# A decay series moved along VectorE's order, and three tiles' router scores computed during a square root

## The reference, cut to what matters

```python
x_r = part of x @ w_in                         # 1280 channels, 10 blocks of 128
xc = causal_dwconv(x_r, conv_r_w) + conv_r_b   # 4 taps
r_gate = sigmoid(block_diag(xc, w_rg_a, b_rg_a))
i_gate = sigmoid(block_diag(xc, w_rg_x, b_rg_x))
log_a = -8 * r_gate * softplus(-rg_lambda)     # the decay; softplus by a series here
a_t, b_t = exp(log_a), sqrt(-expm1(2 * log_a)) * (i_gate * xc)
h_r = linear_recurrence(a_t, b_t)
...
x = layer_norm(ALPHA * x + merged @ w_out)
logits = x @ w_router + b_router               # 16 scores a token
group = argmax over 4 groups of the sum of the two best probabilities
experts = the two best in that group
```

## Time and profile before

| what | value |
|---|---|
| median of 3 runs | 827.77 us (827.19 to 829.04) |
| the profiled execution | 826.91 us |
| its span, first to last instruction | 825.2 us |
| PE busy | 813.2 us, 99% |
| DVE busy | 575.2 us, 70% |
| ACT busy | 455.0 us, 55% |
| POOL busy | 81.9 us, 10% |

### The profile page before, as it was taken

One profiled execution on the slowest core, in us unless ns is written; L12 is line 12 of the kernel. 1 busy time (PEld: TensorE's weight loads), 2 busy tenths in 40 slices (PEclk: granted clock), 3 DMA queues, 4 the chain that ended last, 5 costly groups with the idle time before them and its releaser, 6 DMA issues.

```text
span 825.2 us, 11010 instructions
## 1 busy us (share of the span) xinstructions
PE 813.2 (99%) x3803; PEld 676.4 (82%) x3803; DVE 575.2 (70%) x672; ACT 455.0 (55%) x462; POOL 81.9 (10%) x78
## 2 busy tenths in 40 slices
PE   9999999999999999999999999999999999999996
PEld 8788888888888888888888888888888888888883
DVE  5877445434547886432455688898899989999977
ACT  5655524433466663432332434578787788887842
POOL 1000000100000000000000000551310001100027
PEclk9999999999999999999999999999999999999998
DMA  7232324653233333333532836499999999999692
GB/s 232 81 107 85 102 84 149 202 178 101 77 102 102 89 88 106 98 103 114 172 95 76 332 127 233 138 376 386 419 373 390 392 396 400 392 396 393 255 363 104
DMA packets 112358, 173.51 MB, mean 210 GB/s; under 512 B 7418, under 2 KB 90019, under 8 KB 100550
## 3 DMA queue, kind: packets, MB, share of 16 engines
q1 hardware_dynamic: 106502, 159.80, 54.7%
q0 software_dynamic: 5824, 13.30, 4.2%
HBM read 163.49 MB, written 16.30 MB: 218 GB/s over the span
## 4 chain that ended last, share of the span: by engine, by line
PE 86%; DMA 6%; DVE 5%; issue 1%; ACT 1%; DVEq 0%; SPq 0%; ACTq 0%
PE psA L718 8%; PE psA L720 8%; PE psA L719 8%; PE psB L718 6%; PE psB L719 6%; PE psB L720 6%; PE psA L905 5%; PE psA L907 5%; PE psA L906 5%; DMA est<-in_w_exp_down_dram 5%; DVE elo L1656 2%; PE psB L932 2%; PE psB L930 2%; PE psB L931 2%; PE psD L719 2%; PE psD L718 2%
## 5 line engine op out<-in xcount | busy, mean ns | idle before, releaser
L1656 DVE TENSOR_TENSOR elo<-est,ehi 128x2048 fp32r<-128x2048 f32 x94 | 212.4, 2288 | 26.1 <-ACT ehi L1254 26.0
L1254 ACT ACTIVATE ehi<-est 128x2048 fp32r<-128x2048 f32 x94 | 178.9, 1924 | 53.5 <-DMA est<-in_w_exp_down_dram 36.5
L1441 DVE TENSOR_TENSOR wlo<-wst,whi 128x1024 fp32r<-128x1024 f32 (+1 forms) x75 | 93.9, 1251 | 84.9 <-ACT whi L1081 84.2
L1081 ACT ACTIVATE whi<-wst 128x1024 fp32r<-128x1024 f32 (+1 forms) x75 | 80.9, 1078 | 76.9 <-PE psB L720 30.7
L905 PE MATMUL psA<-ehi,xe_hi 128*128 128x512 f32 x256 | 101.5, 397 | 0.2 <-issue 0.2
L907 PE MATMUL psA<-ehi,xe_lo 128*128 128x512 f32 x256 | 99.9, 390 | 0.0
L906 PE MATMUL psA<-elo,xe_hi 128*128 128x512 f32 x256 | 99.6, 389 | 0.0
L718 PE MATMUL psB<-xT_hi,whi 128*128 128x512 f32 x208 | 81.0, 390 | 0.0
L720 PE MATMUL psB<-xT_hi,wlo 128*128 128x512 f32 x208 | 80.9, 389 | 0.0
L719 PE MATMUL psB<-xT_lo,whi 128*128 128x512 f32 x208 | 80.9, 389 | 0.0
L907 PEld LDWEIGHTS psA<-ehi,xe_lo 128*128 128x128 f32 x256 | 48.0, 188 | 10.4
(11 more groups left out here) (374 smaller groups left out, 1532.7 us busy)
## 6 DMA issues: line engine op xcount, KB each, us to landing
est<-in_w_exp_gate_dram SPq DMA_DIRECT2D x32, 1024.0 KB, 11.0
est<-in_w_exp_up_dram SPq DMA_DIRECT2D x32, 1024.0 KB, 11.4
est<-in_w_exp_down_dram SPq DMA_DIRECT2D x32, 1024.0 KB, 12.9
wst<-in_w_in_dram SPq DMA_DIRECT2D x59, 512.0 KB, 3.9
wst<-in_w_branch_r_dram SPq DMA_DIRECT2D x8, 640.0 KB, 4.3
ys<-zero POOLq DMA_DIRECT2D x8, 512.0 KB, 2.9
wst<-in_w_branch_a_dram SPq DMA_DIRECT2D x8, 512.0 KB, 3.6
o_st<-in_w_out_dram SPq DMA_DIRECT2D x8, 512.0 KB, 4.3
```

The costliest lines, as they stand in the source:

```text
L1081: A(whi[p][:, 0:K, :], wst[p][:, 0:K, :], ACT.Copy).then_inc(w_hi, 1)
L1254: A(ehi[s][:], est[s][:], ACT.Copy).then_inc(gu_hi if s < 4 else d_hi, 1)
L1441: V.tensor_tensor(wlo[p][:, 0:K, :], wst[p][:, 0:K, :], whi[p][:, 0:K, :], ALU.subtract).then_inc(w_lo, 1)
L1656: V.tensor_tensor(elo[s][:], est[s][:], ehi[s][:], ALU.subtract).then_inc(gu_lo if s < 4 else d_lo, 1)
```

## The change

Three edits, all in DVE's order. Ahead of the loop, `decay_first` runs before `rg_rest(0)` and `rg_rest(1)`; `rg_rest(0)` comes behind the first convolution, `xc_rest(0)` ahead of `lo(2)`, `rg_rest(1)` behind `lo(2)`; and `decay_rest` comes behind the second convolution, its remainder, and the drive of block 0. `gates_of` is split in `decays` and `drive`. In the root, the scores of tiles 0 to 2 are computed between the last tile's variance and its reciprocal.

```diff
-            def gates_of(j, p):
+            def decays(j):
+                V.tensor_scalar(_tile(zbuf, j), _tile(zbuf, j), _col(decay[:, 0, :], 0, j), None, ALU.mult)
+
+            def drive(j, p):
                 dve.wait_ge(gate_done, j + 1)
-                V.tensor_scalar(_tile(zbuf, j), _tile(zbuf, j), _col(decay[:, 0, :], 0, j), None, ALU.mult)
                 V.tensor_tensor(_tile(ibuf, j), ig[p][:], xc[p][:], ALU.mult).then_inc(ix_done, 1)
 
-            rg_rest(0, 0)
-            rg_rest(1, 1)
             decay_first()
             conv_rest(0, 0)
+            rg_rest(0, 0)
+            xc_rest(0, 0)
             lo(2, 0)
-            xc_rest(0, 0)
-            decay_rest()
+            rg_rest(1, 1)
             conv_rest(1, 1)
             lo(3, 1)
             xc_rest(1, 1)
-            gates_of(0, 0)
+            drive(0, 0)
+            decay_rest()
+            decays(0)
...
-                    gates_of(2 * i + (p - 1), 1 - p)
+                    dve.wait_ge(gate_done, 2 * i + p)
+                    decays(2 * i + (p - 1))
+                    drive(2 * i + (p - 1), 1 - p)
...
+            def score(t):
+                return V.scalar_tensor_tensor(lb[:, t, :], logit_ps[t], st1[:, t, 18:19],
+                                              shift[:, t, :], ALU.mult, ALU.subtract)
+
             def norm(t):
...
+                if t == TT - 1:
+                    dve.wait_ge(logit_done, TT - 1)
+                    for u in range(TT - 1):
+                        score(u)
                 dve.wait_ge(std_done, t + 1)
...
-            for t in range(TT):
-                dve.wait_ge(logit_done, max(t + 1, TT - 1))
-                ins = V.scalar_tensor_tensor(lb[:, t, :], logit_ps[t], st1[:, t, 18:19],
-                                             shift[:, t, :], ALU.mult, ALU.subtract)
-            chain.link(ins)
+            dve.wait_ge(logit_done, TT)
+            chain.link(score(TT - 1))
```

More of the change, by code:

```diff
@@ L1529, in _ @@
                     xc_rest(2 * i + p, p)
-                    gates_of(2 * i + (p - 1), 1 - p)
+                    dve.wait_ge(gate_done, 2 * i + p)
+                    decays(2 * i + (p - 1))
+                    drive(2 * i + (p - 1), 1 - p)
             chain.n = start + 4 * (KR // 2 - 1)
-            gates_of(KR - 1, 1)
+            dve.wait_ge(gate_done, KR)
+            decays(KR - 1)
+            drive(KR - 1, 1)
             QC = KR * S // 4
@@ L1664, in residual @@
                 V.bn_stats(st1[:, t, 6 * h:6 * h + 6], row).then_inc(stats_done, 1)
+            lb = r16[2]
+            def score(t):
+                return V.scalar_tensor_tensor(lb[:, t, :], logit_ps[t], st1[:, t, 18:19],
+                                              shift[:, t, :], ALU.mult, ALU.subtract)
             def norm(t):
@@ L1764, in _ @@
             ex, iota3 = r16[1], iota_e[:].unsqueeze(1).to_broadcast([P, TT, NE])
-            lb, inside = r16[2], r16[4]
+            inside = r16[4]
             def beats(o, v):
```

## The result

Over 22 executions of each kernel the changed one takes 829.22 us in the median (828.07 to 829.80) and the kernel before 826.69 (826.09 to 829.04). The ratio is 1.0023, with a 95% interval of 1.0017 to 1.0029: slower by 1.9 us, or 1.4 to 2.4. The ratio isn't the quotient of the two medians, which lie 2.53 apart; the means, 829.11 and 827.21, lie 1.90 apart. The forecast was +1.9 and 829.7 us. The three executions that were shown ahead of the prediction lay high, with a median of 827.77. The profiled execution of the changed kernel took 829.5 us, its span 827.8.

The account below looks back on a forecast made before the run. TensorE, busy 99% of the span, was taken to bound the kernel. +2.24 us from the start and -0.33 from the scores made +1.9, added to the 827.77 median: 829.7 us, range 826.6 to 830.9.

Parts of the forecast that it names:

- a queue entry held up by rg_lo(0): SyncE's queue: weight tile 3's load waits behind a reload that needs rg_lo(0); new TensorE stop of about 1.8 us.
- the series without cover: VectorE, second half of the decay series ahead of the third convolution: TensorE stops again for 1.2 us.
- the gain at rg(0): First gate products on TensorE: the 0.82 us hole ahead of them goes, and they start at 22.43.
- the scores: Last tile's root: three scores (0.51 us) leave the chain, reciprocal 0.18 later; net -0.33, bounds -0.51 to 0.
- The issue of tile 3: SyncE issues weight tile 3's load at 21.89, not 17.32, 1.28 us behind the end of rg_lo(0).
- ScalarE's rounding: ScalarE rounds weight tile 3 once its load lands, at 26.0 (25.7 to 27.0), instead of 23.30.
- rg(1) and rg(2): Second and third starts of gate products on TensorE: at 31.0 and 39.1, 0.84 and 2.12 us later than before.
- Nothing late behind the first wait: Rival, chance 0.13: tile 3's weights come in time, third gate products start at 36.4; 827.0 us.
- Only the first new stop: Rival, chance 0.08: second half of the series finds cover, third gate products start at 37.9; 828.4 us.
- The table switch: Rival, chance 0.03: ScalarE's table load costs twice its 1.28 us in its new place; 831.0 us.
- The clock: Rival, chance 0.03: TensorE's clock falls in a 1.8 us stop; one round at 1.2 GHz costs up to 6.8; 836 us.
- The threshold: Whole kernel: 0.2%, or 1.66 us, tells from no change (829.4); slower has 0.54, within 0.43, faster 0.03.

Follow-up runs that it names:

- i1_best: Repeat of e6_best (changed kernel, rg_lo(0) ahead of the series, six of the second half's twelve operations moved earlier); 825.93 us, ratio 0.9990.
- i2_scores: Kernel before with the score edit alone, run again; 826.00 us, ratio 0.9989.
- g2_early: Changed kernel without the score edit, so VectorE's new order at the start alone; 829.44 us, ratio 1.0030.
- g3_spq: Changed kernel with only SyncE's loop altered: both weight tiles loaded ahead of both pairs of gate weights; 825.96 us, ratio 0.9984.
- e5_rg0: Changed kernel with rg_lo(0), the first small remainder of gate weights, back ahead of the series; 825.98 us, ratio 0.9988.
- g4_cover: Changed kernel with the series' second half cut in two, six operations ahead of tile 3's small remainder and six behind it; 827.88 us, ratio 1.0008.
- e6_best: Changed kernel with rg_lo(0) ahead of the series and six of the second half's twelve operations between the remainders of tile 3 and xc(1); 825.95 us, ratio 0.9989.
- h1_before16: Kernel before with 16 filler products instead of 12 on TensorE while the experts are chosen; 826.76 us, ratio 0.9993.
- e7_best8: e6_best with 8 filler products instead of 12 on TensorE while the experts are chosen; 826.62 us, ratio 0.9992.
- h2_before8: Kernel before with 8 filler products instead of 12 on TensorE while the experts are chosen; 827.12 us, ratio 1.0001.

## Why the prediction was right

- **The number and the mechanism.** The mechanism came as it was written: a queue entry held up by rg_lo(0), then the series without cover. That the number came so close is in part luck. The 829.7 was added up from the median of three executions, 827.77, which lies 1.08 above the median of 22, 826.69; the measured 829.22 is 2.53 above the latter. The +1.9 has two terms that were off in opposite directions, the gain at rg(0) and the scores.
- **The gain at rg(0)** came: no hole. Its size of 0.82 was one execution's. In the medians it is worth 0.1 (i1_best against i2_scores), and in the other four profiles with the old order the hole is 0.30 to 0.54. This term was mis-sized; I took the distance between two chains that start from different transfers for a constant. The medians agree: the three rounds of g2_early are 3.15 us longer than three of 6.80, and less 0.82 that would be +2.3; its median is +2.75, which leaves, as an estimate, about 0.4 for this gain.
- **The issue of tile 3** was forecast for 21.89, and is at 21.99 on the clock of the forecast (22.39 - 0.40). ScalarE's rounding was forecast for 26.0: 26.01. g3_spq and e5_rg0 show that nothing else makes the first stop.
- **rg(1) and rg(2)** were forecast for 31.0 and 39.1, and are at 30.94 and 38.93. The terms of VectorE's chain (drive, series, decays, rg_lo, convolution, lo, xc_lo) held within 0.1 each. A little too much was added up along the way: +2.24 in the forecast, +2.10 in the profile.
- **The scores** were forecast at -0.33 and gave -0.50. The step that was off: I let the first score start 0.13 behind the variance and take 0.17 for each, so that they ran past the square root. They start 0.07 behind it, and the reciprocal is 0.50 behind the variance where it was 0.46 before. The lower bound of the forecast, -0.51, was this case.
- **The sum** of the profile: +0.40 for the late start, +2.10, -0.50, +0.48 for the fillers at 1.2 GHz, +0.1 later; together 2.6, the distance of 829.5 from 826.91. Only the second and third are the change's, and they make +1.6 in this pair of profiles. The two halves of the change measured apart make +2.75 - 0.60 = +2.15 in the medians. The forecast of +1.9 lies between.
- **Rivals.** "Nothing late behind the first wait" is what g3_spq and e5_rg0 are, near 826.0; it took another order of the queue or of rg_lo(0) to get there. "Only the first new stop" is what g4_cover would be without the fall of the clock. The table switch cost 1.28 in its new place, and the sigmoid followed at 28.78, 0.02 behind its end: no drain, as in the trace before. The clock didn't fall in the two stops in either profile of the changed kernel, nor in that of g2_early (stops of 0.85 to 1.65 us); in g4_cover, after 2.10 us, it did, and cost 1.6, not the 6.8 that I had set as the utmost.
- **The threshold.** 0.2% of 826.69 is 1.65 us, and the change is +1.9 with an interval of 1.4 to 2.4. So the measurement can't say on which side of the threshold it lies. That it would be so close was in the chances.

## What to carry to other kernels

Before an instruction is moved back behind longer work, list everything its semaphore releases, the DMA queue first: what stands behind that one wait in the queue is held up too, though it needs nothing of it. Work that is moved off one wait needs cover where it lands; here half of the series fitted in VectorE's idle time ahead of xc_lo(1), and all of it together did not fit ahead of the loop. A hole whose two ends depend on different transfers is worth what it is on average, not what one profile shows.

## What the runs showed of the hardware that I had not expected

TensorE's granted clock fell to 1.2 GHz in the middle of the kernel, where the page of the kernel before shows 2.4 GHz up to its last slice. In three profiles (changed, e5_rg0, e6_best) it fell under the router's small products of 16 columns or right behind them, and in h1_before16 under the fillers, some 0.7 us behind them; the engine showed 1.00 busy up to there in all four. In g2_early, e7_best8 and h2_before8 it fell 0.3 to 2.1 us behind the first of the ranks, ahead of which stood 1.36 to 2.35 us of idle time; and in g4_cover behind 2.10 us of idle time at the start. The router's products run in every profile, and stops of 1.44 us (the kernel before), 1.55 (changed) and 1.65 (g2_early, at the start) passed without a fall; what decides is open. What it costs depends on what runs then. Under the fillers it costs nothing up to the moment when they run past the choice (0.2 to 0.9), under the router's products the last score is late too (0.2 to 0.3), and under row products it costs 1.2 to 1.6. A filler is work that must end in time at either clock.
